# Gate and up products of an encoder's feed-forward layers: weight blocks as the stationary operand, both parts of x side by side as the moving one, activations no longer turned on TensorE

## What is computed

```python
def rms_norm(x, g):
    xf = x.astype(jnp.float32)
    y = xf * lax.rsqrt(jnp.mean(xf * xf, axis=-1, keepdims=True) + EPS)
    return (y * g.astype(jnp.float32)).astype(x.dtype)

def swiglu_half_step(h, norm_g, w_gate_up, w_down):
    hn = rms_norm(h, norm_g)
    gate, up = jnp.split(hn @ w_gate_up, 2, axis=-1)
    return h + 0.5 * ((jax.nn.silu(gate) * up) @ w_down)
```

## Time and profile before

| | us |
|---|---|
| median of 3 runs (935.74 to 937.02) | 935.95 |
| the profiled execution | 936.07 |
| its span, first to last instruction | 934.3 |
| TensorE busy (4448 matmuls and as many loads) | 928.7 |
| VectorE, ScalarE, GpSimd busy | 555.6, 461.4, 49.4 |

### The profile page before, as it was taken

How to read it: one execution, slowest core, us unless ns; L and a number is a source line. 1 busy time by engine, 2 the same in 40 slices (tenths; PEclk the granted TensorE clock), 3 DMA queues, 4 the chain that set the end, 5 groups by cost and what they waited for, 6 DMA issues and landing times.

```text
span 934.3 us, 13327 instructions
## 1 busy us (share of the span) xinstructions
PE 928.7 (99%) x4448; PEld 762.8 (82%) x4448; DVE 555.6 (59%) x701; ACT 461.4 (49%) x652; POOL 49.4 (5%) x82
## 2 busy tenths in 40 slices
PE   9999999999999999999999999999999999999998
PEld 5888888887888888888878888888887788888887
DVE  6655454585566555455687545545777765464553
ACT  6644443465545444453464435444666554444441
POOL 2010110003000000000000000000221000000000
PEclk9999999999999999999999999999999999999999
DMA  8786566445137646556356665656433276566541
GB/s 294 256 267 217 172 189 216 159 150 187 46 116 246 219 152 202 190 178 217 100 186 207 217 200 165 207 167 199 141 120 117 67 239 211 169 192 212 158 157 45
DMA packets 136863, 166.98 MB, mean 179 GB/s; under 512 B 10776, under 2 KB 101632, under 8 KB 136832
## 3 DMA queue, kind: packets, MB, share of 16 engines
q1 hardware_dynamic: 135472, 164.67, 55.2%
q0 software_dynamic: 1184, 1.83, 0.8%
q10 hardware_dynamic: 176, 0.07, 0.0%
HBM read 165.48 MB, written 1.05 MB: 178 GB/s over the span
## 4 chain that ended last, share of the span: by engine, by line
PE 98%; DMA 1%; SPq 0%; ACT 0%; issue 0%; DVE 0%
PE ps L1520 22%; PE ps L1522 22%; PE ps L1521 22%; PE ps L1588 8%; PE ps L1590 8%; PE ps L1592 8%; PE ps L1572 2%; PE ps L1455 2%; PE ps L1728 1%; PE ps L1759 1%; DMA h<-in_x_dram 1%; PE ps L1715 1%; PE ps L1696 0%; PE ps L1748 0%; PE ps L1734 0%
## 5 line engine op out<-in xcount | busy, mean ns | idle before, releaser
L984 DVE TENSOR_TENSOR w_lo<-w_raw,w_hi 128x1024 fp32r<-128x1024 f32 x296 | 356.5, 1223 | 144.2 <-ACT w_hi L652 141.7
L652 ACT CAST w_hi<-w_raw 128x1024 fp32r<-128x1024 f32 x296 | 304.1, 1050 | 132.4 <-PE ps L1592 73.2
L1520 PE MATMUL ps<-w_hi,mainT_hi 128*128 128x512 f32 x768 | 305.8, 398 | 0.7 <-DVE mainT_lo L1042 0.5
L1522 PE MATMUL ps<-w_hi,mainT_lo 128*128 128x512 f32 x768 | 299.9, 390 | 0.0
L1521 PE MATMUL ps<-w_lo,mainT_hi 128*128 128x512 f32 x768 | 299.3, 390 | 0.0
L1520 PEld LDWEIGHTS ps<-w_hi,mainT_hi 128*128 128x128 f32 x768 | 144.2, 188 | 32.6 <-DVE w_lo L984 2.1
L1522 PEld LDWEIGHTS ps<-w_hi,mainT_lo 128*128 128x128 f32 x768 | 144.1, 188 | 30.9
L1521 PEld LDWEIGHTS ps<-w_lo,mainT_hi 128*128 128x128 f32 x768 | 144.5, 188 | 28.0
L705 ACT ACTIVATE silu_g<-ps,row_rs 128x256 f32<-128x256 f32 x88 | 41.8, 475 | 229.6 <-PE ps L1522 229.6
L1069 DVE SCALAR_TENSOR_TENSOR act_f<-ps,row_rs,silu_g 128x256 f32<-128x256 f32 x88 | 42.6, 484 | 159.8 <-ACT silu_g L705 159.8
L1588 PE MATMUL ps<-w_hi,actT_hi 128*128 128x512 f32 x320 | 99.1, 391 | 0.0
(11 more groups left out here) (193 smaller groups left out, 661.2 us busy)
## 6 DMA issues: line engine op xcount, KB each, us to landing
w_raw<-in_ffn_w_gate_up_dram SPq DMA_DIRECT2D x352, 256.0 KB, 3.6
w_raw<-in_ffn_w_down_dram SPq DMA_DIRECT2D x176, 256.0 KB, 4.1
w_raw<-in_w_in_dram SPq DMA_DIRECT2D x32, 256.0 KB, 3.3
w_raw<-in_w_out_dram SPq DMA_DIRECT2D x32, 256.0 KB, 3.3
w_raw<-in_w_mem_kv_dram SPq DMA_DIRECT2D x16, 256.0 KB, 3.2
...
```

Of the source, the lines that this page charges most:

```text
L652: ins = nc.scalar.copy(half(w_hi[s], b), half(w_raw[s], b))
L984: ins = nc.vector.tensor_tensor(half(w_lo[s], b), half(w_raw[s], b), half(w_hi[s], b).bitcast(F32), ALU.subtract)
L1520: pe.matmul(dst, x_hi, wh, start=start, stop=False)
L1522: return pe.matmul(dst, x_lo, wh, start=False, stop=stop)
```

## The change

The operands of gate and up change places. A block of 128 rows by 128 features of `w_hi` or `w_lo` is stationary, and x moves. `x_hi` and `x_lo` of a chunk now lie side by side (`both`, 512 columns: 256 tokens of hi, 256 of lo). A chunk, for each block of 128 gate features and 128 up features, takes one product of 512 (`w_hi` with both parts) and one of 256 (`w_lo` with x_hi). `gate_up(c, fb)` now goes over the two blocks fb of 128 features and all 256 tokens. A bank then holds two partial sums; ACT copies the second half of two banks out (`parts`), DVE adds the first halves to them (`sums`), multiplies gate by the row scales, now along the free dimension (`rs_rows`, which TensorE turns once in each stage, `turn_scales`), ACT takes silu, DVE multiplies. The result has features on the partitions, so `turn_act` is gone. The row scale of up is applied in `residual`. In `ffn1` to `ffn3` the first block goes by tiles of tokens for k below 4 (`first_gate_up`, products of 256 and 128). In `ffn0` the turns of the gains and of the scales stand inside the first step. The copies of `kv` go from DVE to ACT and to banks 6 and 7.

```diff
...
+RS_BANK = SUM_BANK + 1
+KV_BANK = GU_BANK + 2
...
+        both = sb("mainT", [P, KC, 2, S], F32R)
+        tr_hi = {n: sb(f"{n}T_hi", [P, KC, S], F32R) for n in ("side", "y")}
+        tr_lo = {n: sb(f"{n}T_lo", [P, KC, S], F32R) for n in ("side", "y")}
+        tr_hi["main"], tr_lo["main"] = both[:, :, 0, :], both[:, :, 1, :]
+        gate_up_f = sb("gate_up_f", [P, 2, 2, S])
+        silu_g, act_f = gate_up_f[:, 0, :, :], gate_up_f[:, 1, :, :]
...
-            def silu(f, c, t, norm):
-                s, used = UNIT[f"ffn{f}", "gate"][1]
-                if t == 0:
+            def parts(f, c, fb):
+                if fb == 0:
                     act.wait_ge(gu_done, f * STEPS + c + 1)
                 else:
+                    s, used = UNIT[f"ffn{f}", "gate"][1]
                     act.wait_ge(weights_used[s], (used + c) * 2 + 2)
-                if isinstance(c, int) and c == 0:
-                    act.wait_ge(row_scaled, row_scaled_no(norm, t))
-                nc.scalar.activation(silu_g[:, t, :], ps[:, GU_BANK + t, 0:FB], ACT.Silu,
-                                     scale=row_scale(norm, t)).then_inc(silu_ready, 1)
-            def actT_high(e):
-                act.wait_ge(act_turned, e + 1)
...
+                nc.scalar.copy(gate_up_f[:, :, fb, :],
+                               ps[:, GU_BANK + 2 * fb:GU_BANK + 2 * fb + 2, S:2 * S]).then_inc(parts_copied, 1)
+            def silu(f, c, fb):
+                act.wait_ge(gate_ready, (f * STEPS + c) * 2 + (fb + 1))
+                nc.scalar.activation(silu_g[:, fb, :], silu_g[:, fb, :], ACT.Silu).then_inc(silu_ready, 1)
+            def scale_rows(f):
+                act.wait_ge(rs_turned, f + 1)
+                nc.scalar.copy(rs_rows, ps[:, RS_BANK, 0:S]).then_inc(rs_ready, 1)
+            def actT_high(f, c):
+                act.wait_ge(act_ready, (f * STEPS + c) * 2 + 2)
...
                 nc.scalar.copy(actT_hi[:, :, :, :].rearrange("p c t n -> p (c t n)"),
-                               ps[:, TR_BANK, :]).then_inc(actT_hi_ready, 1)
+                               act_f[:, :, :].rearrange("p c n -> p (c n)")).then_inc(actT_hi_ready, 1)
...
+                def first_step():
+                    if f == 0:
+                        high(name, gate[0], 0, (0,), turn=1)
+                    scale_rows(f)
+                    if f == 0:
+                        act.wait_ge(gains_turned, 2)
+                        nc.scalar.copy(gain_col[:, FIRST_GAINS * KC:GAINS * KC],
+                                       ps[:, RS_BANK, S:S + (GAINS - FIRST_GAINS) * KC]).then_inc(gains_ready, 1)
+                    parts(f, 0, 0)
+                    silu(f, 0, 0)
+                    high(name, gate[0], 0, (1,) if f == 0 else (0, 1), turn=1)
+                    high(name, gate[1], 1, (0,), turn=1)
+                    if f == 0:
+                        parts(f, 0, 1)
+                        silu(f, 0, 1)
+                    high(name, gate[1], 1, (1,), turn=1)
+                    if f > 0:
+                        parts(f, 0, 1)
+                        silu(f, 0, 1)
...
                 last = STEPS - 1
+                actT_high(f, last - 1)
                 high(name, UNIT[name, "down"], None, turn=last - 1)
-                silu(f, last, 0, norm)
-                actT_high(e0 + last - 1)
+                parts(f, last, 0)
+                silu(f, last, 0)
                 high(name, UNIT[name, "end"], None)
-                silu(f, last, 1, norm)
                 if FOLLOWING[name] is not None:
                     high_unit(FOLLOWING[name], 0)
...
+                parts(f, last, 1)
+                silu(f, last, 1)
+                act.wait_ge(act_ready, (e0 + last) * 2 + 2)
                 nc.scalar.copy(endT_hi[:, :, :, :].rearrange("p c t n -> p (c t n)"),
-                               ps[:, TR_BANK + 1, :]).then_inc(actT_hi_ready, 1)
+                               act_f[:, :, :].rearrange("p c n -> p (c n)")).then_inc(actT_hi_ready, 1)
...
             high_first(2)
             high_first(3)
+            split("H0", 0, 1)
             high_first(4)
-            split("H0", 0, 1)
-            row_sum("H0", 0)
             high_first(5)
             split("H0", 1, 1)
+            row_sum("H0", 0)
             high_first(6)
             high_first(7)
             row_sum("H0", 1)
...
+            def sums(f, c, fb):
+                bank = GU_BANK + 2 * fb
+                n = (f * STEPS + c) * 2 + (fb + 1)
+                dve.wait_ge(parts_copied, n)
+                nc.vector.tensor_tensor(silu_g[:, fb, :], ps[:, bank, 0:S], silu_g[:, fb, :],
+                                        ALU.add).then_inc(gate_summed, 1)
+                nc.vector.tensor_tensor(act_f[:, fb, :], ps[:, bank + 1, 0:S], act_f[:, fb, :],
+                                        ALU.add).then_inc(up_summed, 1)
                 if isinstance(c, int) and c == 0:
+                    dve.wait_ge(rs_ready, f + 1)
+                dve.wait_ge(gate_summed, n)
+                nc.vector.tensor_tensor(silu_g[:, fb, :], silu_g[:, fb, :], rs_rows, ALU.mult).then_inc(gate_ready, 1)
+            def gated(f, c, fb):
+                dve.wait_ge(silu_ready, (f * STEPS + c) * 2 + (fb + 1))
+                nc.vector.scalar_tensor_tensor(out=act_f[:, fb, :], in0=act_f[:, fb, :], scalar=0.5,
+                                               in1=silu_g[:, fb, :], op0=ALU.mult, op1=ALU.mult).then_inc(act_ready, 1)
...
+                sums(f, last, 1)
+                if after is not None:
+                    low_unit(FOLLOWING[name], 0, (0,))
+                gated(f, last, 1)
+                if after is not None:
+                    low_unit(FOLLOWING[name], 0, (1,))
+                act_low(endT_lo, e0 + last)
...
+            def turn_scales(f, norm):
+                pe.wait_ge(row_scaled, row_scaled_no(norm, NT - 1))
+                for t in range(NT):
+                    mm = pe.transpose(ps[:, RS_BANK, t * P:(t + 1) * P], row_scale(norm, t).to_broadcast([P, P]), ident[:, :])
+                mm.then_inc(rs_turned, 1)
+            def gate_products(units, k, fb, tile, start, stop):
+                s, _ = units[k // 4]
+                tokens = slice(0, S) if tile is None else slice(tile * P, (tile + 1) * P)
+                for j in range(2):
+                    dst = ps[:, GU_BANK + 2 * fb + j, :].rearrange("p (c t) -> p c t", c=2)
+                    cols = slice(j * FB + fb * P, j * FB + (fb + 1) * P)
+                    wh, wl = w_hi[s][:, k % 4, cols], w_lo[s][:, k % 4, cols]
+                    if not stop:
+                        pe.matmul(dst[:, :, tokens], wh, both[:, k, :, tokens], start=start, stop=False)
+                    mm = pe.matmul(dst[:, 0, tokens], wl, both[:, k, 0, tokens], start=False, stop=False)
+                    if stop:
+                        mm = pe.matmul(dst[:, :, tokens], wh, both[:, k, :, tokens], start=False, stop=True)
+                return mm
+            def first_piece(k, fb):
                 s, _ = UNIT["ffn0", k // 4]
...
+                if fb == 0:
+                    for t in range(NT):
+                        if k == 0:
+                            pe.wait_ge(first_x_lo[t], 1)
+                        elif k in (2, 4):
+                            pe.wait_ge(split_lo[t][k // 4], split_no("H0"))
                     if k % 2:
-                        pe.wait_ge(lo_ready[s], kk // 2 + 1)
+                        pe.wait_ge(lo_ready[s], k % 4 // 2 + 1)
                     else:
                         pe.wait_ge(first_lo, k // 2 + 1)
...
+                mm = gate_products(UNIT["ffn0", "gate"], k, fb, None, k == 0, k == KC - 1)
+                if fb == 1 and k % 2 == 1:
                     mm.then_inc(weights_used[s], 1)
...
+                if fb == 0 and k == KC - 1:
                     mm.then_inc(gu_done, 1)
             def first_step():
...
                 turn_first(0, 1)
                 turn_first(1, 1)
-                first_piece(0, 1)
-                first_piece(1, 0)
-                first_piece(1, 1)
...
+                for k in range(KC - 2):
                     first_piece(k, 0)
-                    first_piece(k - 1, 1)
+                    first_piece(k, 1)
+                    if k == 1:
+                        turn_h("H0", 0, 1)
+                    elif k == 2:
+                        turn_h("H0", 1, 1)
+                first_piece(KC - 2, 0)
+                pe.wait_ge(gains_landed[1], 16 * (len(GAIN_ROWS) - 1))
+                pe.transpose(ps[:, RS_BANK, S:S + (GAINS - FIRST_GAINS) * KC], gain_rows[1],
+                             ident[0:(GAINS - FIRST_GAINS) * KC, 0:(GAINS - FIRST_GAINS) * KC]).then_inc(gains_turned, 1)
+                turn_scales(0, "H0")
+                first_piece(KC - 1, 0)
+                first_piece(KC - 2, 1)
                 first_piece(KC - 1, 1)
...
+                def gate_up(c, fb, hook=None):
+                    if not isinstance(c, int) or c > 0:
```

(58 more changed lines are left out.)

242 lines of the change are left out of this document (115 added, 127 removed).

## The result

| | before | changed |
|---|---|---|
| median of 4 runs, us | 936.49 | 948.35 (947.74 to 949.06) |
| profiled execution, its span | 936.07, 934.3 | 947.74, 945.9 |
| TensorE busy, instructions | 928.7, 4448 | 928.2, 5033 |

The ratio is 1.0127 with an interval of [1.011, 1.0145]: slower, by 11.9 us. The forecast was 942.6, with a range of 932 to 954. Between the two profiled executions the difference is 11.67 us, and the sum had 6.5.

A forecast was written before the change was run, and what follows sets the result against it. The prediction took TensorE's instruction issue as the bound, busy 928.7 of 934.3 us. Terms A to F, -21.4 + 12.2 + 1.0 + 3.5 + 12.2 - 1.0 = +6.5 us on 936.07, gave 942.6, range 932 to 954.

The forecast's parts named there:

- term E: First step of `ffn0`: TensorE waits 6.7 us for the gains, stalls follow, loop starts at 52.0; +12.2 us, bounds 5 and 15.
- Term A: Turns of the activations go: 44 groups of four, 0.49 us each, some 0.44 at a stage's end; -21.4 us.
- Term B: Gate and up products of other widths, same columns; a product of 256 takes 0.120 us; +12.2 us, bounds +0.8 to +148.
- Rival 1: Gate and up: a product of 256 costs only columns and share, 0.112 to 0.114 us; 932.5 us, not slower; chance 0.17.
- rival 3: Gate and up: alternating widths never settle to even spacing, 2816 x 5 ns = +14 us, 957 us; chance 0.10.
- Term D: End of a stage: TensorE stalls 1.55, 1.0 and 1.0 us ahead of the end products; +3.5 us, bounds 0 and 6.
- Terms C: Turning the row scales: two turns of 0.109 us in each of four stages, with a met wait; +1.0 us.
- F: Small stalls in `ffn1` to `ffn3`, for `w_lo` and bank 4, go; -1.0 us, bounds -1.2 and +1.5.
- Cover: Loop steps: VectorE's added sums (+2.1 us) and ScalarE's copies (+1.2 us) are hidden by TensorE's products.

The follow-up runs named there:

- Experiments 1: The changed kernel with TensorE's wait for and turn of the gains moved behind gate_up(1, 0) of `ffn0`, ScalarE's copy with them: 939.75 us, 1.0036.
- 4: The kernel before with only the turn of the gains moved into the first step, ahead of chunk 7, and ScalarE's copy ahead of its first silu: 944.58 us, 1.0088.
- 7: The changed kernel with the four gains DMAs issued by GpSimd ahead of the row-scale roots, the turn left ahead of chunk 7: 940.10 us, 1.0041.
- experiment 8: The changed kernel with 29 unused bf16 products of 512 ahead of TensorE's wait for the gains: 947.30 us, 1.0113.
- Experiment 12: The kernel before with each group of four turns of the activations made twice into the same bank: 955.33 us, 1.02.
- experiment 10: Experiment 1's kernel with each product of 512 split into two of 256 with the same weights: 957.89 us, 1.0229.
- Experiments 3: Experiment 1's kernel with a chunk's two products of 512 first and its two of 256 behind them: 938.35 us, 1.0022.
- 6: Experiment 5's kernel without the grouping, the product of 256 ahead of that of 512 in each pair, chunk 0 apart: 936.95 us, 1.0004.
- Experiment 5: Experiment 3's kernel with ScalarE's and VectorE's work reordered at the ends of stages and the start of `ffn0`: 935.18 us, 0.9987.

## Why the prediction was nearly right

**The direction and its cause: term E, right.** The forecast had TensorE at the wait at 19.4, idle for 6.7 us until 26.1, and the loop at 52.0. The trace has 19.3, 6.78, 26.04 and 52.40. Experiments 1, 4 and 7 show by three ways that this one wait is worth 8.2 to 8.6 us. Of the rest of the 12.75, most stays as waits behind ScalarE's and VectorE's queues: in kernel 1, TensorE still waits 0.9 us for `mainT`, 2.1 for `w_lo` and 0.7 for `sideT_lo`. That the 52.0 came so close is in part luck, since errors compensated. The last gains DMA was issued at 20.34, not 21.1, and landed 5.65 us later, not 5.0. The stalls for `w_lo` were 0.8 and 0.9 us with the load behind them, not 2.0 and 1.2, 1.5 us less. Part of that is the slow clock, which delayed TensorE as well: with the clock kept up (experiment 8) the first is 1.4. And the slow stretch cost 1.65 us, which the sum did not have. That clock stood beside the sum in a sentence on the Trainium skill ("TensorE: Matmul & The Clock Gate", The HAM clock gate), which has the array fall to 1.2 GHz after idling. The trace agrees with that (0.52, and 1.00 with the wait filled); up to the loop it was worth some 0.9 us, as experiment 8 shows.

**Term A, right.** Experiment 12 prices four turns at 19.3 / 44 = 0.44 us; the 0.05 of slower products did not come a second time, and is not shown by itself. (The forecast's "43 groups of 0.49" should be 40, with four of 0.44; its sum of 21.4 is that of 40 and four.)

**Term B, the step that was mis-sized.** The price of 0.120 for a product of 256 is right where the spacing is even (experiment 10, and block 1). Rival 1, a price of 0.112 to 0.114, falls. But the forecast took the even spacing for all pairs. Block 0 of each step takes 353 ns a pair, and a step 16.66 us in place of 16.53. Some 0.1 of these 0.13 us are block 0, the rest is block 1 and the down products, which take 5.46 in place of 24 x 0.2267 = 5.44. Two of the 44 steps lie ahead of the loop of `ffn0` and are in term E. Over the other 42 it is 5.5 us if the first steps of the stages lose as much as those of the loop, and that is the error of the forecast: 5.5, with 0.4 for E and -0.7 for D, gives 5.2, and the error is 11.67 - 6.5 = 5.2. It is a milder form of rival 3, 3 ns a product in block 0 and almost nothing in block 1, in place of 5 in both. Experiments 3 and 6 show that the pattern changes with the order of widths. Why one block settles and the other does not stays open.

**Term D, right in place, a little high.** The idle times were 1.20, 0.54 and 0.55 us, with the unhidden load 1.37, 0.71 and 0.71, together 2.8 in place of 3.5. Experiment 5 takes them away by order alone; it is 3.2 us faster than kernel 3 by the medians and 2.6 by the spans (936.6 and 934.0).

**Terms C and F, not contradicted.** The changed kernel waits for `w_lo` twice in all, both times in `ffn0`, so the delay of the earlier trace rows is gone as forecast. Neither term was tried by itself; what the other terms leave of the error is under 0.2 us, which leaves room for errors of theirs that compensate.

**Cover.** VectorE went from 59% to 67% and ScalarE from 49% to 53%, and in the loop TensorE waits for neither, as forecast.
